# One pick in four of the expert sum handed from TensorE to ScalarE and GpSimd

## The reference, cut to what matters

```python
def peer_block(h, w_peer_q, sub_keys, expert_u, expert_v):
    ...                                     # 8 heads, top 16 of 128 x 128 product keys each
    eidx = jnp.take_along_axis(cidx, sel, axis=-1)
    g = jax.nn.softmax(best, axis=-1).astype(h.dtype)
    a = jax.nn.gelu(jnp.einsum('thkd,td->thk', expert_u[eidx], h), approximate=False)
    return jnp.einsum('thk,thkd->td', g * a, expert_v[eidx])
```

## Time and profile before

| | |
|---|---|
| runs | 4040.15, 4043.93 and 4044.23 us |
| the profiled execution | 4033.68 us, span 4031.5 us |
| TensorE, matmul | 3336.6 us busy, 83% |
| VectorE | 2542.3 us, 63% |
| ScalarE | 1439.1 us, 36% |
| GpSimd | 1153.7 us, 29% |
| gathers | 1056, 1107.36 MB, 67.6% of the time of the 16 DMA engines |
| granted TensorE clock, mean | 0.899 |

### The profile page before, as it was taken

The page is one execution under the profiler, slowest core; times in us unless marked ns, Lnnn a source line. Parts: engine busy times, 40 slices in busy tenths (PEclk is TensorE's granted clock), DMA queues, the critical chain, the costliest instruction groups (busy, mean ns, idle before and its releaser), DMA issues.

```text
span 4031.5 us, 36425 instructions
## 1 busy us (share of the span) xinstructions
PE 3336.6 (83%) x10788; PEld 1820.2 (45%) x10788; DVE 2542.3 (63%) x5428; ACT 1439.1 (36%) x4284; POOL 1153.7 (29%) x1316
## 2 busy tenths in 40 slices
PE   7987979947789998777778989877888878887887
PEld 4653337824445544333444445433444434465431
DVE  2104531477855699677766677994777677745874
ACT  1012221127822333356662233333444444422343
POOL 0000000033322343433333334442333233323442
PEclk9998968978899999887889999988988889887999
DMA  2011124449999998999999999999999898999999
GB/s 107 16 58 32 38 63 123 129 153 407 409 361 357 403 387 330 366 405 402 413 374 420 426 406 403 373 357 380 358 361 373 332 370 334 389 383 416 426 420 387
DMA packets 230961, 1274.64 MB, mean 316 GB/s; under 512 B 45356, under 2 KB 61292, under 8 KB 95157
## 3 DMA queue, kind: packets, MB, share of 16 engines
q0 software_dynamic: 152064, 1107.36, 67.6%
q1 hardware_dynamic: 76980, 160.67, 11.3%
q10 hardware_dynamic: 1728, 4.39, 0.3%
HBM read 1256.76 MB, written 15.56 MB: 316 GB/s over the span
## 4 chain that ended last, share of the span: by engine, by line
PE 35%; DMA 24%; DVE 14%; issue 6%; ACT 4%; POOL 1%; SPq 1%; POOLq 0%; ACTq 0%; DVEq 0%
DMA tl_uv<-in_uv,tl_idx 21%; PE tl_y L1002 14%; PE tl_f L1236 7%; DVE tl_uv L1567 3%; PE tl_f L1247 3%; PE tl_f L1262 2%; DVE tl_acc L1554 2%; DMA X<-in_krope 2%; PE tl_f L1062 1%; DVE tl_picked L1651 1%; DMA w_tail<-in_w_merge 1%; PE tl_f L1172 1%; PE tl_f L1195 1%; PE tl_f L1114 1%; POOL tl_uv L926 1%
## 5 line engine op out<-in xcount | busy, mean ns | idle before, releaser
L1567 DVE CUSTOM_DVE_ANT_0 tl_uv<-tl_uv,tl_h 128x1024 f32<-128x1024 f32 x1056 | 1272.3, 1218 | 766.0 <-DMA tl_uv<-in_uv,tl_idx 734.5
L1002 PE MATMUL tl_y<-tl_uv,tl_diag 128*128 128x512 f32 (+1 forms) x2828 | 1454.9, 657 | 247.5 <-ACT tl_diag L1283 243.1
L926 POOL DMA_INDIRECT tl_uv<-in_uv,tl_idx x1056 | 1039.9, 985 | 1927.8 <-PE tl_y L1002 1466.3
L1002 PEld LDWEIGHTS tl_y<-tl_uv,tl_diag 128*128 128x128 f32 (+1 forms) x2828 | 548.5, 205 | 983.6 <-issue 564.4
L1311 ACT ACTIVATE tl_ge<-tl_a 128x1 f32<-128x1 f32 x1056 | 209.2, 198 | 1174.9 <-DVE tl_a L1567 1151.0
L1554 DVE SCALAR_TENSOR_TENSOR tl_acc<-tl_uv,tl_w,tl_acc 128x1024 f32<-128x1024 f32 x341 | 436.9, 1281 | 62.6 <-ACT tl_w L1295 62.3
L1295 ACT ACTIVATE tl_w<-tl_ge,tl_weight 128x1 f32<-128x1 f32 x1024 | 301.5, 294 | 33.2
L1283 ACT ACTIVATE tl_diag<-K,tl_w 128x128 f32<-128x128 f32 (+1 forms) x707 | 281.3, 398 | 48.8 <-PE tl_y L1002 26.4
L1236 PE MATMUL tl_f<-H,w_tail 128*128 128x384 f32 (+2 forms) x1024 | 268.6, 419 | 31.4 <-DMA w_tail<-in_w_merge 30.2
L1262 PE MATMUL tl_f<-H,w_tail 128*128 128x384 f32 (+2 forms) x1024 | 265.5, 414 | 8.4 <-DVE H L1748 8.4
L938 POOL TENSOR_TENSOR tl_cand<-tl_tv 128x48 f32<-128x48 f32 (+5 forms) x128 | 27.7, 247 | 778.0 <-DVE tl_ti L1599 778.0
(11 more groups left out here) (216 smaller groups left out, 3250.2 us busy)
## 6 DMA issues: line engine op xcount, KB each, us to landing
w_tail<-in_w_merge SPq DMA_DIRECT2D x96, 512.0 KB
w_tail<-in_w_peer SPq DMA_DIRECT2D x64, 576.0 KB
tl_uv<-in_uv,tl_idx POOLq DMA_INDIRECT x1056
w_tail<-in_w_mix SPq DMA_DIRECT2D x32, 512.0 KB
X<-in_cache SPq DMA_DIRECT2D x64, 128.0 KB
w_conv<-in_w_conv SPq DMA_DIRECT2D x4, 1536.0 KB, 10.0
X<-in_x SPq DMA_DIRECT2D x8, 536.0 KB, 7.2
o_y<-tl_acc ACTq DMA_DIRECT2D x8, 512.0 KB
```

The source lines that it names most:

```text
L926: pool.indirect_dma_start(UV[:, u % RING, :], None, d["uv"], bass.IndirectOffsetOnAxis(ap=which, axis=0)).then_inc(landed[u % RING], 16)
L1002: mm = pe.matmul(Y[0:m, half * 512:(half + 1) * 512], DG[:, (pe_count[u] - 1) % DIAGS, 0:m], UV[:, u % RING, D + half * 512:D + (half + 1) ...
L1567: dve.tensor_tensor_reduce(UV[:, u % RING, 0:D], UV[:, u % RING, 0:D], HP[:], 1.0, 0.0, ALU.mult, ALU.add, A[:, t % 2, i:i + 1]).then_inc( ...
```

## The change

Within tiles 0 to 7, picks 10, 14, 18, ... 118 (28 a tile, 224 in all) no longer go to TensorE; all of them had gone there before, since the units of VectorE are odd. ScalarE writes v * w over v in the slot, or, for a tile's first such pick, into a new buffer `PACC`. GpSimd adds the slot to PACC (216 adds), in its own queue, behind the issue of the gather seven units later. VectorE's end of tile gets a second addition, ACC = PACC + ACC, and `copied` comes behind it.

```diff
+        PACC = sb("pool_acc", [P, D])
...
+        def by_pool(u):
+
+            return chunk_of(u // PICK) + 1 < NCH and 8 <= u % PICK < PICK - 8 and u % 4 == 2
+
         def by_dve(u):
 
             c = chunk_of(u // PICK) + 1
-            if c == NCH or u % PICK < 8:
+            if c == NCH or u % PICK < 8 or by_pool(u):
                 return False
...
                     if by_dve(v):
                         pool.wait_ge(used_dve, dve_units[v])
+                    elif by_pool(v):
+                        pool.wait_ge(used_pool, pool_units[v])
                     else:
                         pool.wait_ge(used, pe_count[v])
...
+                if u >= RING - 1 and by_pool(u - RING + 1):
+                    accumulate(u - RING + 1)
+
+            def accumulate(u):
+                t, i = divmod(u, PICK)
+                if u == first_pool[t]:
+                    return
+                pool.wait_ge(scaled, pool_units[u] - t - 1)
+                pool.wait_ge(used_pool, pool_units[u] - 1)
+                pool.tensor_tensor(PACC[:], PACC[:], UV[:, u % RING, D:2 * D], ALU.add).then_inc(used_pool, 1)
...
-                if by_dve(u):
+                if not by_pe(u):
                     return
                 pe.wait_ge(diag, pe_count[u])
...
+            def scale(u):
+                t, i = divmod(u, PICK)
+                v, w = UV[:, u % RING, D:2 * D], WP[:, t % 2, i:i + 1]
+                act.wait_ge(weighed, u + 1)
+                if u == first_pool[t]:
+                    if t:
+                        act.wait_ge(copied, t)
+                    act.activation(PACC[:], v, ACT.Copy, scale=w).then_inc(used_pool, 1)
+                else:
+                    act.activation(v, v, ACT.Copy, scale=w).then_inc(scaled, 1)
+
             def diagonal(u):
-                if by_dve(u):
+                if by_pool(u):
+                    scale(u)
+                if not by_pe(u):
                     return
...
-                dve.tensor_tensor(ACC[:], Y[:], ACC[:], ALU.add).then_inc(copied, 1)
+                dve.tensor_tensor(ACC[:], Y[:], ACC[:], ALU.add).then_inc(added, 1)
+                dve.wait_ge(added, t + 1)
+                dve.wait_ge(used_pool, pool_units[u])
+                dve.tensor_tensor(ACC[:], PACC[:], ACC[:], ALU.add).then_inc(copied, 1)
```

More of the change, by code:

```diff
@@ L696, in tail_stage @@
          ifset, cand, paired, marked, diffed, picked, finished, ranked, expo, normed, gset, spread, fourfold, turned, dot,
-         gelu, weighed, diag, used, used_dve, copied) = (
+         gelu, weighed, diag, used, used_dve, used_pool, copied) = (
             sem(n) for n in ("gain_in", "ya_in", "stored", "tables", "proj", "act_took", "dve_took", "mset", "squared",
@@ L700, in tail_stage @@
                              "finished", "ranked", "expo", "normed", "gset", "spread", "fourfold", "turned", "dot",
-                             "gelu", "weighed", "diag", "used", "used_dve", "copied"))
+                             "gelu", "weighed", "diag", "used", "used_dve", "used_pool", "copied"))
         (tbl_in, dec_in, wk_in, wv_in, newk, ssd, rooted, step, logits, maxed, powered, inverse, probs, av_stored) = (
@@ L704, in tail_stage @@
                              "powered", "inverse", "probs", "av_stored"))
+        added, scaled = sem("added"), sem("scaled")
         page_in = [sem(f"page_in{s}") for s in range(2)]
@@ L807, in by_dve @@
             return u < due(c, END, 0) and u % 8 == 7
-        pe_count = list(itertools.accumulate(0 if by_dve(u) else 1 for u in range(UNITS)))
+        by_pe = lambda u: not by_dve(u) and not by_pool(u)
+        pe_count = list(itertools.accumulate(1 if by_pe(u) else 0 for u in range(UNITS)))
+        pool_units = list(itertools.accumulate(1 if by_pool(u) else 0 for u in range(UNITS)))
         dve_units = list(itertools.accumulate(1 if by_dve(u) else 0 for u in range(UNITS)))
-        first_sum = {t: next((u for u in range(unit(t, 0), unit(t, picks(t))) if by_dve(u)), None) for t in range(NP)}
+        first_of = lambda t, mine: next((u for u in range(unit(t, 0), unit(t, picks(t))) if mine(u)), None)
+        first_sum = {t: first_of(t, by_dve) for t in range(NP)}
+        first_pool = {t: first_of(t, by_pool) for t in range(NP)}
         def follow(unit_of):
```

## The result

The changed kernel takes 4098.32 us (median of four runs, 4095.72 to 4104.16) against 4042.04 us before: a ratio of 1.0148, with a 95% interval of 1.0123 to 1.0174. (The ratio is that of the means; one of the four runs before is low, 4028.37 us, and the medians give 1.0139.) The forecast was 4004 us, with a range up to 4095. The time is near rival B's milder size (4088); how much of B's reasoning came true is said further down.

What follows compares the result with a forecast made beforehand. DMA bounds the attention stages and second merge, TensorE 1128-1435 us, VectorE the first ranking, no single engine decode. -20 - 28 - 7 + 3 + 5 + 5 + 2 = -40 us gave 4004 us; range 3935 to 4095.

Steps and rivals of the forecast that it cites:

- rival B: Decode and rankings: GpSimd's addition becomes the slot's late release; slower, 4088 us at 0.97 us for each of 102; chance 0.30.
- What bounds, and the first merge: 1128-1435 us: TensorE is the bound; 18 moved picks take 33 us off it, of which 20 us gained.
- Relief in decode, 28 us: Decode, 2780-3531 us: 52 picks leave TensorE, 57 us of the chain of waits; half taken, 28 us gain.
- The 7 us of the second ranking: Second ranking and the mix before it, 2323 to 2700 us: 7 of 20 us idle DMA time gained.
- ScalarE, 3 us: ScalarE's scale takes 1.15 us, 0.75 more per moved pick, delaying queued gelu and copies; bounds 0 and 39, cost 3 us.
- The chain does not name ScalarE's pick work: Reason given for taking ScalarE's longer scale near no cost, 3 us: the chain of waits does not name that work.
- GpSimd's addition, 5 us: GpSimd's queue: 216 additions of 1.94 us before later gathers and marks; bounds 0 and 213 us, cost 5 us.
- one is exchanged for the other: At the gather u + 8: the old wait for TensorE's matmuls, 1.83 to 2.05 us, gives way to the addition.
- The "saturated" attention stages: 873 to 1128 and 1690 to 2126 us: DMA share 0.99 to 1.01, so no gain, and these stages keep their length.
- The lock, 5 us: Rankings and decode: VectorE instructions with two SBUF inputs and GpSimd's exclude each other; 0 to 99 us, cost 5 us.
- The end of a tile, 2 us: Tile ends: one more VectorE addition before `copied`, 11 us on TensorE over 8 tiles; cost 2 us.

Runs made afterwards that it cites:

- experiment 1: Changed kernel with ScalarE freeing the slot by a bare semaphore, no scale and no GpSimd addition (TensorE's relief alone): 4028.35 us, 0.9961 of the kernel before.
- experiment 5: Relief-alone kernel (no scale, no addition), with TensorE running two same-size matmuls on a constant per moved pick, waiting for nothing: 4035.74 us, 0.9965 of the kernel before.
- experiment 2: Changed kernel with ScalarE's scale, which frees the slot itself, but without GpSimd's additions: 4044.99 us, 1.0000 of the kernel before.
- experiment 6: Changed kernel with ScalarE freeing the slot and GpSimd adding a scratch buffer to itself in the same queue places: 4090.09 us, 1.0097 of the kernel before.
- experiment 3: Changed kernel with GpSimd's addition but without ScalarE's scale: 4075.36 us, 1.0080 of the kernel before.
- experiment 7: Changed kernel with GpSimd's addition over 512 of the 1024 columns: 4065.64 us, 1.0047 of the kernel before.
- experiment 4: Changed kernel with VectorE's accumulation reading its third operand from PSUM, so without the VectorE-GpSimd lock: 4091.14 us, 1.0116 of the kernel before.
- experiment 9: Changed kernel with GpSimd's picks only in the first merge and mix (units 85 to 159, 15 picks): 4029.38 us, 0.9960 of the kernel before.
- experiment 11: Kernel before, with every fourth pick of units 85 to 159 given to VectorE, nothing more to ScalarE or GpSimd: 4030.06 us, 0.9956 of the kernel before.

## Why the prediction was wrong, step by step

- **What bounds, and the first merge: right.** 33 us less TensorE work was to give 20; it gave 16 in the change, 17.6 with the relief alone. The work taken away was counted too high: 15 moved picks fall on units 85 to 159 and not 18, and TensorE's busy time in the stage fell by 26 us (252.08 to 225.69).
- **Relief in decode, 28 us: wrong, the largest miss of the gain.** I gave TensorE's pick work 18.7% of the chain and let part of it go. Nothing of it came: decode took 750.4 us with the relief alone (experiment 1), against 736 to 751 where nothing was changed in it, and 738 when TensorE stayed busy but waited for none of these picks (experiment 5). The failed step is the reading of a share of the chain as time that goes away with the work. The relieved TensorE was also granted a lower clock, 36 us more for the same trunk matmuls, and the clock stood in no term of the sum; how much of decode's length it costs stays open. The 7 us of the second ranking did not come either (262.5 against 262.3 us with the relief alone).
- **ScalarE, 3 us: mis-sized.** Its duration was right to 2 ns (1.148 us); its weight on the path was 17 us for the whole scale (experiment 2 over 1), some 11 us, an estimate by length, for the 0.75 us of this term. "The chain does not name ScalarE's pick work" was a poor reason. A likely one for the cost, which no run sets apart: TensorE waits for ScalarE's trunk items, and these stand behind the scales.
- **GpSimd's addition, 5 us: the step that turned the sign.** The term was 5 us; the addition cost 39 us as time in the queue alone (experiment 6) and 47 as a whole without the scale (experiment 3). The duration was 2.37 us and not 1.94, above the value taken and inside the ends. The Trainium skill (GPSIMD Engine Reference, Elementwise — side-by-side cycle accounting) was nearer: half of its 4497 ns for 2048 elements is an estimate of 2.25 us. The step that failed is "one is exchanged for the other": TensorE's matmuls had run beside the issue of gathers, the addition runs in place of them. It has the queue to itself for 2.6 us, and the gather behind it takes 0.35 us longer on average than without the lock. I had compared only rates: four gathers and an addition of 2.37 us are 1.8 us a unit, against 2.7, which is enough on average. But slots come free in bursts: in the kernel before, 409 gathers went out directly behind another. That each burst is now handed out more slowly fits the timeline and experiments 6 and 7, and was not measured by itself. The "saturated" attention stages were only just saturated: they lost 6 and 15 us between the two profiles.
- **The lock, 5 us: mechanism right, size not contradicted.** 7 us by the medians, 13 by the ratios, with an uncertainty as large. I had put VectorE's loss at 0.3 us an addition; it is 0.32 us an accumulation, 109 us in all or 0.5 us an addition, and nearly all of it beside the path. That the gather's issue is stretched too I had not seen.
- **The end of a tile, 2 us:** TensorE's wait before the residual rose from 28.1 to 36.8 us in seven tiles. Experiment 1 has the same 36.8 us, so they are in its 4028 us; no run prices them on the path.
- **The rivals.** B had a part of the mechanism, the addition that delays the next gather. Its name for it, the slot's late release, is not the main part (experiment 6), the lock is small (experiment 4), and it left out the attention stages, which lost as well. The additions cost 53 us by the times (4098 over experiment 2's 4045) and 60 by the ratio, over 216, so 0.25 to 0.28 us each and not 0.97 for 102 of them. That was enough to decide, since the gain was 16 us and not 55. That 4088 lies near the measured time is partly luck: both terms of that sum were too large.

## What to carry to other kernels

An in-order queue that issues the bottleneck's transfers can be part of the bottleneck though it is mostly idle: GpSimd's queue had 1928 us of idle time before, and 216 additions of 1.91 us that nobody waited for still cost 39 us. Comparing average rates gives no price for work put into such a queue. Here the relief of TensorE paid only in the stage that it bounded. Moving work there alone made the kernel faster by 0.4%, and VectorE, which already did such work, served as well as ScalarE and GpSimd together (experiments 9 and 11). When relief makes TensorE idle more, look at the granted clock of the work that stays. And read a stage's length from more than one execution before explaining 15 us of it.

## What the runs showed of the hardware

- GpSimd's addition of two float32 SBUF tiles took 2.36 us for 1024 columns and 1.28 us for 512, 2.1 ns a column with 0.2 us fixed; with both inputs the same tile 1.91 us. The bf16 rows of the kernel before had given 1.70 ns.
- Issues of an indirect gather directly behind an addition took 1.31 us on average, 1.66 in the case shown, while VectorE's accumulations had two SBUF inputs, and 0.96 us when these had one input in PSUM. Without any addition, in the kernel before, issues that overlapped an accumulation took 1.17 us and the others 0.94. An accumulation beside an addition took up to 4.13 us in place of 1.28.
- The granted clock over the whole kernel fell from 0.899 to 0.84 when TensorE's busy time fell from 83% to 75%, and stood at 0.893 with matmuls on a constant in place of the moved ones.
